# Modulation vectors of two later layers summed on VectorE beside the feed-forward products, instead of in PE's steps in the mixing stages

## The reference, cut to what matters

```python
mod_l = jax.nn.silu(c) @ ada_w[l] + ada_b[l]          # c: the latent tokens' condition, 1024
mod_c = jax.nn.silu(c_ctx) @ ada_w[l] + ada_b[l]      # the context tokens' condition
sh1, sc1, g1, sh2, sc2, g2, sh3, sc3, g3 = ...        # nine vectors of 1024 each
xl = post_norm_2(xl, 0.5 * g1 * swiglu_2(modulate_2(xl, sh1, sc1), ffn1_w_in[l], ffn1_w_out[l]))
hl = modulate_2(xl, sh2, sc2)
yc, yl = even_mixer(hc, hl, ...) or odd_mixer(hc, hl, ...)
xl = post_norm_2(xl, g2 * yl)
xl = post_norm_2(xl, 0.5 * g3 * swiglu_2(modulate_2(xl, sh3, sc3), ffn2_w_in[l], ffn2_w_out[l]))
```

## Time and profile before

| | |
|---|---|
| median of 3 runs | 3052.46 us (3048.05 to 3054.0) |
| profiled execution's own time | 3042.79 us |
| its span in the trace | 3041.0 us, mean granted TensorE clock 0.966 |
| PE busy | 2835.1 us (93%) |
| VectorE / ScalarE / POOL busy | 1264.7 / 1011.2 / 233.2 us |
| read from HBM | 532.54 MB, 175 GB/s over the span |

### The profile page before, as it was taken

One profiled execution on the slowest core, in us unless ns is written; L12 is line 12 of the kernel. 1 busy time (PEld: TensorE's weight loads), 2 busy tenths in 40 slices (PEclk: granted clock), 3 DMA queues, 4 the chain that ended last, 5 costly groups with the idle time before them and its releaser, 6 DMA issues.

```text
span 3041.0 us, 39431 instructions
## 1 busy us (share of the span) xinstructions
PE 2835.1 (93%) x17014; PEld 2131.3 (70%) x17014; DVE 1264.7 (42%) x1815; ACT 1011.2 (33%) x1436; POOL 233.2 (8%) x277
## 2 busy tenths in 40 slices
PE   6999899899899889999889989999999999998998
PEld 4854689744434368888667367888878888786998
DVE  4766545511111143333475345333353333435554
ACT  4533444311111142222453224222242222435543
POOL 0025460200000000000030000000000000200000
PEclk8999999899999989999999989999999999999999
DMA  6469756499999942322352542232322323321463
GB/s 245 141 222 332 243 153 180 157 415 421 421 421 421 421 148 87 104 95 84 102 212 68 209 151 70 84 110 87 94 90 87 114 82 98 134 90 42 132 188 97
DMA packets 330186, 536.23 MB, mean 176 GB/s; under 512 B 14324, under 2 KB 291732, under 8 KB 294036
## 3 DMA queue, kind: packets, MB, share of 16 engines
q1 hardware_dynamic: 330004, 533.63, 49.5%
HBM read 532.54 MB, written 1.05 MB: 175 GB/s over the span
## 4 chain that ended last, share of the span: by engine, by line
PE 77%; DMA 12%; DVE 6%; ACT 4%; issue 1%; SPq 0%; POOL 0%; DVEq 0%; ACTq 0%; POOLq 0%
PE ps L186 76%; DMA HF<-in_w_ed 3%; DMA raw_few<-in_w_ed 2%; DMA ALF<-in_w_ed 2%; DMA LF<-in_w_ed 2%; DVE LR L241 1%; DVE ar L241 1%; ACT ar L311 1%; ACT HR L311 1%; DMA RAW<-in_ada_w 1%; DMA RAW<-in_w_ed 1%; PE ps L192 1%; DVE X L241 1%; DMA ALF<-in_w_ada 1%; DVE ar L251 0%
## 5 line engine op out<-in xcount | busy, mean ns | idle before, releaser
L186 PE MATMUL ps<-AH,HR 128*128 128x512 f32 (+1 forms) x2488 | 878.6, 353 | 38.0 <-DVE AL L241 21.9
L186 PE MATMUL ps<-AL,HR 128*128 128x512 f32 (+1 forms) x2488 | 870.8, 350 | 0.0
L186 PE MATMUL ps<-AH,LR 128*128 128x512 f32 (+1 forms) x2488 | 870.4, 350 | 0.0
L241 DVE TENSOR_TENSOR LR<-RAW,HR 128x2048 fp32r<-128x2048 f32 (+3 forms) x232 | 486.7, 2098 | 569.0 <-ACT HR L311 559.4
L311 ACT ACTIVATE HR<-RAW 128x2048 fp32r<-128x2048 f32 (+3 forms) x232 | 404.1, 1743 | 618.1 <-PE ps L186 581.1
L186 PEld LDWEIGHTS ps<-AH,HR 128*128 128x128 f32 x2488 | 480.3, 193 | 108.8 <-ACT ar L311 14.1
L186 PEld LDWEIGHTS ps<-AL,HR 128*128 128x128 f32 x2488 | 480.5, 193 | 58.1
L186 PEld LDWEIGHTS ps<-AH,LR 128*128 128x128 f32 x2488 | 479.4, 193 | 59.5
L241 POOL TENSOR_TENSOR ar<-ar 128x384 f32<-128x384 f32 (+7 forms) x124 | 138.2, 1122 | 1244.6 <-DMA ar<-in_cst 1021.3
L186 PE MATMUL ps<-ar 64*64 64x64 f32 (+8 forms) x1270 | 161.2, 332 | 35.3 <-DVE ar L241 19.8
L251 DVE SCALAR_TENSOR_TENSOR X<-ps,mod,X 128x256 f32<-128x256 f32 x152 | 67.4, 480 | 236.1 <-PE ps L186 236.1
(11 more groups left out here) (220 smaller groups left out, 3414.8 us busy)
## 6 DMA issues: line engine op xcount, KB each, us to landing
RAW<-in_ada_w SPq DMA_DIRECT2D x72, 1024.0 KB, 6.7
RAW<-in_f1i SPq DMA_DIRECT2D x44, 1024.0 KB, 5.1
RAW<-in_f2i SPq DMA_DIRECT2D x44, 1024.0 KB, 5.1
RAW<-in_w_in SPq DMA_DIRECT2D x32, 1024.0 KB, 5.6
RAW<-in_w_ada SPq DMA_DIRECT2D x16, 1024.0 KB, 6.5
RAW<-in_w_eg SPq DMA_DIRECT2D x15, 1024.0 KB, 21.8
HF<-in_w_ed SPq DMA_DIRECT2D x15, 1024.0 KB, 26.7
LF<-in_w_ed SPq DMA_DIRECT2D x15, 1024.0 KB, 24.8
```

Of the source, the lines that this page charges most:

```text
L186: return self.e.matmul(o, w, x, start=start, stop=stop)
L241: return self.e.tensor_tensor(o, a, b, op) if self.e else NOTHING
```

## The change

The job list after `later` holds only the first 16 tiles of layer 0's matrix (`lead2`, 8 steps), so that 24 steps are left after the first block's beginning. In the SSD stage they have a place only in the rounds 2, 5 and 8 of each group. All calls of `step` in the gated linear attention and in the latent attention are gone.

The other 128 tiles (56 of layer 0, 72 of layer 1; of the last 32 only the latent tokens' vector is wanted) become 32 blocks of 4 tiles, 512 columns, in nine groups. Three groups (12 blocks) lie in f1i0, four (12 blocks) in f2i0, two (8 blocks, one vector) in f1i1, none in f2i1. For a block, POOL issues two loads of 1 MB into the two halves of `f.sq` (`aside_pool`). VectorE multiplies each of the eight 128 x 512 parts with the column of the condition vector and adds up in `f.part`, for one or two vectors (`aside_dve`), in portions put behind its work for each tile of the hidden layer and of the down pass. PE sums over the partitions with a matrix that has one column of ones (`aside_pe`); ScalarE copies the group's row (`aside_act`), PE turns it (`aside_turn`), VectorE adds bias and gates (`aside_mod`). In these networks PE keeps bank 0 for that, up to the second pass's down part.

```diff
+SPARE = [r % 3 == 2 for r in range(8 + LAG)]
...
-        self.ada2 = [Job("ada_w", i, 0, 72, 2, self.v("ada_b", 72 * i, 72), self.mod2[i], GATES, 3 + 5 * i)
-                     for i in range(2)]
+        self.lead2 = Job("ada_w", 0, 0, 16, 2, self.v("ada_b", 0, 72), self.mod2[0], GATES, 3)
...
+        g = Aside.groups((0, 16, 4, 2), (0, 32, 4, 2), (0, 48, 4, 2),
+                         (0, 64, 2, 2), (1, 0, 2, 2), (1, 8, 4, 2), (1, 24, 4, 2),
+                         (1, 40, 4, 1), (1, 56, 4, 1))
...
-    S.jobs = [K.later, K.ada2[0]]
+    S.jobs = [K.later, K.lead2]
...
-            T.step()
+            T.step(SPARE[r])
...
+def aside_pool(G, K, f):
+    for b in f.blocks:
+        g = b.group
+        for h in range(2):
+            c, at = 2 * b.i + h, (g.at + 4 * b.m) * 128
+            if c >= 2 * f.blocks[0].i + 2:
+                G.wait_ge(*K.dve.of("aside chunk", c - 2))
+            src = K.dram["ada_w"][g.layer][512 * h:512 * h + 512, at:at + 512].rearrange("(k p) n -> p k n", p=128)
+            G.dma(f.chunks[h], src).then_inc(K.aside[h], 16)
...
+def aside_dve(V, K, f):
+    dve = K.dve
+    for b in f.blocks:
+        for k in range(8):
+            h, i = k // 4, 2 * b.i + k // 4
+            w = f.chunks[h][:, k % 4, :]
+            if k % 4 == 0:
+                V.wait_ge(K.aside[h], 16 * (b.i + 1))
+            if k == 0 and b is not f.blocks[0]:
+                V.wait_ge(*K.pe.of("aside", b.i - 1))
+            for v in range(b.group.nv):
+                c, part = K.CS[:, k, 2 + v:3 + v], f.part[:, v, :]
+                if k:
+                    V.wait_ge(*dve.of("aside part", b.i, k - 1, v))
+                    V.stt(part, w, c, part, MUL, ADD).then_inc(*dve("aside part", b.i, k, v))
+                else:
+                    V.ts(part, w, c, None, MUL).then_inc(*dve("aside part", b.i, k, v))
+            if k % 4 == 3:
+                dve.note("aside chunk", i)
+            yield k
...
+def aside_pe(T, K, f, b):
...
+    T.wait_ge(*K.dve.of("aside part", b.i, 7, g.nv - 1))
+    for v in range(g.nv):
+        for q in range(4):
+            r = T.mm(K.banks[0][32 * q:32 * q + 32, 128 * b.m:128 * b.m + 128], K.hot[:, 1 - v:33 - v],
+                     f.part[:, v, 128 * q:128 * q + 128], v == 0, v == g.nv - 1)
+    r.then_inc(*K.pe("aside", b.i))
...
+def aside_turn(T, K, g):
...
+    for m in range(g.count):
+        r = T.mm(b[:, 16 * m:16 * m + 16].rearrange("p (q v) -> p q v", q=4), K.mrow[:, 128 * m:128 * m + 128],
+                 K.ident[:, :].rearrange("p (q c) -> p q c", q=4)[:, :, 0:4], True, True)
...
+    def summed(self, *at):
+        i = {(0, 2 * p): p - 1 for p in range(1, 6)}
+        i.update({("down", 1): 5, ("down", 5): 6})
+        i.update({(1, 12 + 2 * p): 7 + p for p in range(5)})
...
 def ffn_pe(T, K, f):
...
+    T.lo = 1 if f.blocks else 0
...
                 r.then_inc(*pe(tag, "up", m0 + i))
+                if i == 0:
+                    aside(p, m0)
             pe.note("w", T.ring.name, j)
+        if first:
+            if f.turned("end"):
+                aside_turn(T, K, f.turned("end"))
+            T.lo = 0
...
 def ffn_dve(V, K, f):
...
                  SUB).then_inc(*dve(tag, "lo", m))
+            if i and f.turned(p, m - 1):
+                aside_mod(V, K, f.turned(p, m - 1))
+            aside(4)
...
             residual_dve(V, K, down, m, f.X, n, f.gate, [K.act.of(tag + "h", "hi", 7)])
+            if not first:
+                aside((0, 2, 2, 2, 2, 3, 3, 2)[m])
...
 def ffn_pool(G, K, f):
     meet(G, K, f.prev)
+    aside_pool(G, K, f)
...
-        self.steps = (3, 3, 2, 2, 2, 0, 0)
-        self.pace = (2, 2, 2) + 12 * (1,) + 4 * (0,)
...
-    T.lo, T.jobs = 1, [K.ada2[1]]
```

More of the change, by code:

```diff
@@ L2451, in after_pool, with __init__, groups @@
     K.pool.note("lead end")
+class Block:
+    def __init__(self, i, group, m):
+        self.i, self.group, self.m = i, group, m
+        self.last = m == group.count - 1
+class Aside:
+    def __init__(self, i, layer, at, count, nv, first):
+        self.i, self.layer, self.at, self.count, self.nv = i, layer, at, count, nv
+        self.blocks = [Block(first + m, self, m) for m in range(count)]
+    @staticmethod
+    def groups(*specs):
+        out, first = [], 0
+        for i, (layer, at, count, nv) in enumerate(specs):
+            out.append(Aside(i, layer, at, count, nv, first))
+            first += count
+        return out
@@ new lines, in aside_mod @@
+def aside_mod(V, K, g):
+    bias, dst = K.v("ada_b", 72 * g.layer, 72), K.mod2[g.layer]
+    rows = K.ps("aside turned", g.i)[:, 0:16 * g.count].rearrange("p (t v) -> p t v", v=4)
+    V.wait_ge(*K.pe.of("aside turned", g.i))
+    for t in range(0, 4 * g.count, 8):
+        at = g.at + t
+        V.stt(dst[:, at:at + 8, :], rows[:, t:t + 8, 0:2], GATES.get(at // 8, 1.0),
+              bias[:, at:at + 8].unsqueeze(2).broadcast_to([128, 8, 2]), MUL, ADD).then_inc(*K.dve("aside mod", g.i))
+    K.free(K.dve, "aside turned", g.i)
@@ new lines, in aside_pe @@
+def aside_pe(T, K, f, b):
+    g = b.group
+    if b.m == 0:
+        row, held = T.hold(0, "aside row", g.i)
+        for h in held:
+            T.wait_ge(*h)
+    T.wait_ge(*K.dve.of("aside part", b.i, 7, g.nv - 1))
[4 more added lines that the diff above has]
+    r.then_inc(*K.pe("aside", b.i))
+    if b.last:
+        K.pe.note("aside row", g.i)
@@ new lines, in aside_act @@
+def aside_act(S, K, g):
+    S.wait_ge(*K.pe.of("aside row", g.i))
+    n = 128 * g.count
+    S.act(K.mrow[:, 0:n], K.ps("aside row", g.i)[:, 0:n], ACT.Copy).then_inc(*K.act("aside row", g.i))
+    K.free(K.act, "aside row", g.i)
+def aside_turn(T, K, g):
+    b, held = T.bank("aside turned", g.i)
+    for h in held:
+        T.wait_ge(*h)
+    T.wait_ge(*K.act.of("aside row", g.i))
+    for m in range(g.count):
+        r = T.mm(b[:, 16 * m:16 * m + 16].rearrange("p (q v) -> p q v", q=4), K.mrow[:, 128 * m:128 * m + 128],
+                 K.ident[:, :].rearrange("p (q c) -> p q c", q=4)[:, :, 0:4], True, True)
+    r.then_inc(*K.pe("aside turned", g.i))
@@ L2468, in __init__, with done, turned @@
         self.lead = nxt and Lead(*nxt, self.X, self.tmp)
+        self.groups, self.blocks = groups, [b for g in groups for b in g.blocks]
+        self.chunks, self.part = [self.sq[:, 4 * i:4 * i + 4, :] for i in range(2)], self.tmp
         self.passes = ((0, 12, f"{self.tag}d0"), (12, 10, f"{self.tag}d1"))
         ctx.close()
+    def summed(self, *at):
+        i = {(0, 2 * p): p - 1 for p in range(1, 6)}
+        i.update({("down", 1): 5, ("down", 5): 6})
+        i.update({(1, 12 + 2 * p): 7 + p for p in range(5)})
+        n = i.get(at, -1)
+        return self.blocks[n] if 0 <= n < len(self.blocks) else None
+    def done(self, *at):
+        b = self.summed(*at)
+        return b.group if b and b.last else None
+    def turned(self, *at):
+        before = {(0, 2 * p): (0, 2 * p - 2) for p in range(1, 6)}
+        before.update({("down", 1): (0, 10), ("down", 5): ("down", 1), (1, 12): ("down", 5)})
+        before.update({(1, 12 + 2 * p): (1, 10 + 2 * p) for p in range(1, 5)})
+        before["end"] = (1, 20)
+        return self.done(*before[at if len(at) > 1 else at[0]]) if (at if len(at) > 1 else at[0]) in before else None
 def ffn_pe(T, K, f):
@@ L2475, in ffn_pe, with aside @@
     ready = row_ready(K, tag + "h")
-    for first, cnt, down in f.passes:
+    def aside(*at):
+        if f.turned(*at):
+            aside_turn(T, K, f.turned(*at))
+        if f.summed(*at):
+            aside_pe(T, K, f, f.summed(*at))
+    T.lo = 1 if f.blocks else 0
+    for p, (first, cnt, down) in enumerate(f.passes):
         for m0 in range(first, first + cnt, 2):
@@ L2553, in ffn_dve, with aside @@
     meet(V, K, f.prev)
-    for first, cnt, down in f.passes:
+    parts = aside_dve(V, K, f)
+    def aside(n):
+        for _ in range(n):
+            next(parts, None)
+    for p, (first, cnt, down) in enumerate(f.passes):
         for m in range(first, first + cnt):
@@ L2568, in ffn_dve @@
                  SUB).then_inc(*dve(tag, "lo", m))
+            if i and f.turned(p, m - 1):
+                aside_mod(V, K, f.turned(p, m - 1))
+            aside(4)
+        if first and f.turned("end"):
+            aside_mod(V, K, f.turned("end"))
         before = centred_dve(V, K, down, f.X, n)
```

51 lines of the change are left out of this document (21 added, 30 removed).

## The result

The changed kernel takes 3058.4 us (median of 12 runs, 3047.6 to 3065.4) against 3049.5 for the kernel before on the same chips: ratio 1.0025, interval 1.0013 to 1.0037. Forecast were 3014 us and a range of 2992 to 3046. The profiled execution took 3047.6 us, its span 3045.6, 4.6 more than before. It is the shortest of the twelve, with a mean granted clock of 0.960 where the other eleven have 0.952 to 0.958, so what the medians add to the profile's difference lies in executions that were not profiled.

The account below looks back on a forecast made before the run. PE, busy 93% of the span, was taken as the bound, alone in the feed-forward networks. −20 − 15 − 31 + 28 = −38 us against the profiled 3042.8 gave 3005, or 3014 from the runs' median; range 2992 to 3046.

Parts of the forecast that it names:

- SSD, −20: SSD stage: removing 28 conditioning steps was to save 20 us, bounds −24 and −9.
- POOL becomes the bound: SSD stage: without steps POOL, at 2.63 us a round, sets the pace, giving 35.5 us a group.
- Gated linear attention, −15: Gated linear attention: removing 18 steps and waits for landing loads was to save 15 us, bounds −8 to −18.
- Latent attention, −31: Latent attention: removing 18 steps was to make the stage 47 us instead of 78.5, bounds 0 and −34.
- the 4 us for a stretch at 1.2 GHz: Latent attention: 4 us added to the stage's forecast time for a stretch at the lower clock.
- The latent window at 0.50: Latent attention: a granted clock of 0.50 in this window was to show the forecast wrong.
- rival of the clock: Latent attention: the loop stays at 1.2 GHz, its −31 becomes 0, net −7, 3045 us; chance 0.12.
- Networks, +28: Feed-forward networks: 32 added blocks (19.1 us) and nine turns (8 to 9) on PE, bounds +19 and +45.
- time for a Silu, so nothing: Feed-forward networks: the bank taken away costs nothing, as the previous pair's gate products end 5.4 us early.
- The constant tile is filled in the set-up: nothing: Set-up: filling the new constant tile was to cost nothing.
- VectorE fits: Feed-forward networks: VectorE's 20.5 us per tile pair fits PE's 22.4, so its added operations cost nothing.
- Late loads, the slower rival: Feed-forward networks: POOL-issued chunk loads land late, at 25 us each adding 269, about 3280 us; chance 0.09.

Follow-up runs that it names:

- e4_early: e3_banks with the three conditioning steps of each SSD group in rounds 0, 1 and 2 instead of 2, 5 and 8: 3028.0 us, ratio 0.9932.
- e7_last: e4_early with the fourth SSD group's two last steps in rounds 0 and 8: 3026.6 us, ratio 0.9923.
- e6_fill: e3_banks plus two unneeded fp32 matmuls of 256 columns in rounds 0, 1 and 2 of each SSD group: 3053.8 us, ratio 1.0010.
- e5_spread: e3_banks with SSD steps in rounds 0 and 1, in the fourth group in rounds 0, 1, 4, 6 and 8: 3023.9 us, ratio 0.9918.
- e8_apart: e7_last with SSD steps in rounds 0, 1, 2 (groups one, two), 0, 1 (three), 0, 4, 8 (four): 3022.9 us, ratio 0.9929.
- e2_shift: The kernel before with an unused tile of 33 columns (132 bytes in each partition) added: 3057.8 us, ratio 1.0034.
- e1_align: The changed kernel with its new constant tile 64 columns (256 bytes) wide instead of 33 (132 bytes): 3042.8 us, ratio 0.9984.
- e3_banks: e1_align with all eight banks kept for the networks' first two tile pairs and the last group turned outside bank 7: 3028.2 us, ratio 0.9940.

## Why the prediction was wrong, point by point

- **SSD, −20: failed, −5.** "POOL becomes the bound" and 35.5 us a group were right, at 1.00: 35.3 to 35.8 in five groups of e4_early and e7_last. The failing step is that PE's own work in a group was taken at the clock of before: 92 us without steps, so some 114 with the 19 steps and three turns that stay. It took 134, at 0.75 to 0.87, and PE, not POOL, still made more than half of the chain. The clock was a rival, but only in the latent loop. That the steps had held it up here as well is borne out by the eight groups with steps in the first rounds; by e6_fill not any work does. The Trainium skill, "TensorE: Matmul & The Clock Gate", section "HAM oscillation — how this bites in real kernels", describes a clock that falls again and again where short bursts of matmuls stand between waits for loads. The trace agrees as to the fall, 0.50 in the first rounds of a group; the waits here are for VectorE and POOL, not for loads.
- **Gated linear attention, −15: right, −15.9.** In 1546 to 1606 VectorE is now busy 57.9 of 60 us, and nearly all of PE's waits end with VectorE, none with a load.
- **Latent attention, −31: mechanism right, size off, −23.** The mis-sized term is the 4 us for a stretch at 1.2 GHz: the clock is 0.50 from 1692 to 1712 and at 1.00 only from 1717 on, and the stage took 55.1 us where 47 had been worked out, 8 more. The latent window at 0.50 was one of the prediction's own signs of being wrong, and its rival of the clock came true in part. The bounds 0 to −34 held.
- **Networks, +28: failed, +59.** Three steps, by the runs. (1) "time for a Silu, so nothing": the 5.4 us hold for pairs whose two tiles end one after the other, not for the first pair of f2i0 and f1i1, and the turned rows' bank was not followed at all: 13.3 us. (2) "The constant tile is filled in the set-up: nothing": its place in memory cost 10 to 12 us. (3) The rest, 36.0, is the term itself, above 28 and inside its bounds: by PE's timeline a block of two vectors takes 0.83 us instead of 0.66, one of one vector 0.58 instead of 0.41. The block pushes two products apart by 0.66 us, as forecast, but the products behind it come at 0.34 and 0.23 to 0.24 us for a while. Blocks and the nine turns (0.81 to 0.89 us, 0.44 the short ones) make 31 of the 36; the same networks are 32 to 34 longer than before in e5_spread to e8_apart. In the timeline after, a block between the products at 1130.39 and 1131.28:

```profile
1130.39 0.39 PE L187 MATMUL ps<-AH,LR 128*128 128x512 f32 x1
1130.70 0.65 PE L187 MATMUL ps<-arf1i,hot 128*32 128x128 f32 x16
1131.28 0.50 PE L187 MATMUL ps<-AH,HR 128*128 128x512 f32 x1
1131.62 0.40 PE L187 MATMUL ps<-AL,HR 128*128 128x512 f32 x1
1131.86 0.40 PE L187 MATMUL ps<-AH,LR 128*128 128x512 f32 x1
```

- **VectorE fits: right.** In 1102 to 1228 PE is busy 126 of 126 us with the clock at 1.00, VectorE 94.4, 75 in 100 where 85 had been forecast. The additions took 747 ns, 753 forecast. No wait of PE there was VectorE's cut. The window, and the page's group of the additions:

```profile
1102.00:1228.00 126.00, 126.00 (x623) 102.75 (x623) 94.37 (x122) 34.98 (x35) 7.48 (x10) 1.00 0.60 192
```

```profile
L252 DVE SCALAR_TENSOR_TENSOR arf1i<-arf1i,CS 128x512 f32<-128x512 f32 x224 | 155.6, 747 | 1.7
```

- **Late loads, the slower rival: did not happen.** 5.6 us to landing from POOL's queue. The Trainium skill, "SBUF — State Buffer", section "🔬 SBUF: two separate sides", has loads issued by POOL held up while VectorE runs in its fast two-port mode; beside additions of 747 ns nothing of it shows. The time came out slower by another way, which no rival had: a clock in the SSD stage, a bank order and a tile's place.

With −20 and −31 at their real sizes and +59 for +28, the sum is −5 − 16 − 23 + 59 = +15 against the −38 forecast; −10 in untouched stages makes the 4.6 of the profile. The forecast's three networks and its SSD stage were wrong by 31 and 15 us, and the gated linear attention alone came out at its size. The range's low end, 2992, follows from none of the prediction's sums: the terms' bounds give 2995.

## What to carry to other kernels

Work that fills PE's waits can also hold its clock, as the steps did in the SSD stage: before taking it out of a stage, price what is left at both levels of the clock, and look for the stretch where PE would be thin. When a bank is taken away, follow the rotation by hand through each first and last iteration, where products end together or a bank is held by number, not through the steady loop alone. And watch where a new small tile puts the tiles behind it: 256 bytes did no harm here and 132 did; a tile declared last would move none. Compare the mean time of one matmul, form by form, before and after.

## What was not expected of the hardware

A matmul of 512 columns that reads the hidden layer took, with the tiles 132 bytes further on, 397 ns instead of 389 in a kernel otherwise unchanged (e2_shift; in the changed kernel they come every 0.234 us instead of 0.227); moved by 256 bytes it took 389 again (e1_align), and the up products stayed at 0.227 us in all of them. One group of the SSD stage, the second, took 35.3 us at a granted clock of 1.00 (e4_early, e7_last), 36.7 at 0.91 (e3_banks) and 38.5 at 0.82 (the changed kernel), with as many steps in each. And 64 loads of 1 MB issued by POOL beside a VectorE that was 75% busy landed in 5.6 us (median), where SP's loads of 1 MB for the same networks took 6.6 and 5.2.
